# Later activation of the second layer's conditions, and three modulation chunks moved to later phases

## The reference

```python
m_lat = adaln_params(c, w_ada[i], b_ada[i])            # silu(c) @ w_ada + b_ada, six vectors of 1024
m_ctx = adaln_params(c_ctx[None], w_ada[i], b_ada[i])
a_lat = modulate_2(rms_norm(h_lat), m_lat[0], m_lat[1])
o_lat = mixer(a_ctx, a_lat)
h_lat = h_lat + m_lat[2] * o_lat
h_lat = h_lat + m_lat[5] * swiglu(modulate_2(rms_norm(h_lat), m_lat[3], m_lat[4]), ...)
```

## Time and profile before

| | |
|---|---|
| median of 3 runs | 1454.56 us (1452.75 to 1456.83) |
| the profiled execution, span | 1454.6 us |
| the profiled execution's own time | 1454.56 us, one of the three |
| PE busy | 1403.6 us, 96% of the span |
| DVE busy | 848.5 us, 58% |
| ACT busy | 659.0 us, 45% |
| POOL busy | 840.2 us, 58% |
| mean granted TensorE clock | 0.993 of full speed |

### The profile page before, as it was taken

How to read it: one execution, slowest core, us unless ns; L and a number is a source line. 1 busy time by engine, 2 the same in 40 slices (tenths; PEclk the granted TensorE clock), 3 DMA queues, 4 the chain that set the end, 5 groups by cost and what they waited for, 6 DMA issues and landing times.

```text
span 1454.6 us, 21621 instructions
## 1 busy us (share of the span) xinstructions
PE 1403.6 (96%) x8272; PEld 1172.3 (81%) x8272; DVE 848.5 (58%) x1638; ACT 659.0 (45%) x1070; POOL 840.2 (58%) x672
## 2 busy tenths in 40 slices
PE   5999999999999999999999999999999999999998
PEld 2978789999988888546878888888888866888887
DVE  3798667776676689688675333321126768554522
ACT  3555665455453133684342232232226386544442
POOL 1533427998864444675444554544446530699997
PEclk9999999999999999999999999999999999999999
DMA  9748516777775652010445555533333320365664
GB/s 365 288 164 309 195 50 212 248 258 241 243 259 194 202 192 80 31 44 15 174 174 182 195 202 185 193 122 96 102 107 102 110 94 16 118 200 188 187 187 135
DMA packets 71207, 242.01 MB, mean 166 GB/s; under 512 B 7488, under 2 KB 12992, under 8 KB 70720
## 3 DMA queue, kind: packets, MB, share of 16 engines
q1 hardware_dynamic: 68688, 236.63, 48.1%
q10 hardware_dynamic: 2416, 4.00, 0.9%
HBM read 238.50 MB, written 1.05 MB: 165 GB/s over the span
## 4 chain that ended last, share of the span: by engine, by line
PE 52%; DVE 4%; ACT 1%; issue 0%; POOL 0%; DVEq 0%; ACTq 0%
PE bank L731 9%; PE bank L737 9%; PE bank L732 9%; PE bank L593 8%; PE bank L594 4%; PE bank L584 2%; PE bank L586 1%; PE bank L585 1%; PE bank L592 1%; PE cond_a L1124 1%; PE bank L1124 1%; DVE h_both L2239 1%; PE bank L1132 1%; PE cond_a L1185 1%; PE bank L1144 1%; PE cond_b L1144 1%
## 5 line engine op out<-in xcount | busy, mean ns | idle before, releaser
L2010 POOL TENSOR_TENSOR w_lo<-raw,w_hi 128x512 fp32r<-128x512 f32 (+2 forms) x610 | 776.8, 1302 | 581.1 <-ACT w_hi L1466 572.9
L1466 ACT ACTIVATE w_hi<-raw 128x1024 fp32r<-128x1024 f32 (+3 forms) x300 | 307.9, 1029 | 582.7 <-PE bank L737 375.2
L731 PE MATMUL bank<-h_both,w_hi 128*128 128x512 f32 (+1 forms) x1000 | 323.1, 340 | 1.2 <-ACT w_hi L1466 1.2
L732 PE MATMUL bank<-h_both,w_hi 128*128 128x512 f32 (+1 forms) x1000 | 322.5, 340 | 0.0
L731 PEld LDWEIGHTS bank<-h_both,w_hi 128*128 128x128 f32 x1000 | 188.3, 188 | 22.9 <-ACT w_hi L1466 1.4
L732 PEld LDWEIGHTS bank<-h_both,w_hi 128*128 128x128 f32 x1000 | 188.3, 188 | 21.3
L737 PE MATMUL bank<-h_both,w_lo 128*128 128x512 f32 (+1 forms) x1000 | 198.1, 340 | 0.0
L737 PEld LDWEIGHTS bank<-h_both,w_lo 128*128 128x128 f32 x1000 | 160.4, 188 | 21.4 <-POOL w_lo L2010 0.2
L2124 DVE CUSTOM_DVE_ANT_0 ada_junk<-ada_w,cond_a 128x1024 bf16<-128x1024 f32 x128 | 153.5, 1215 | 15.1 <-DVE work L2687 8.1
L2106 DVE TENSOR_TENSOR hidden_both<-work,hidden_both 128x256 fp32r<-128x256 f32 (+1 forms) x66 | 58.5, 886 | 135.0 <-ACT hidden_both L1547 135.0
L593 PE MATMUL bank<-h_both,w_hi 128*128 128x512 f32 x345 | 122.8, 394 | 0.0
(11 more groups left out here) (487 smaller groups left out, 2544.1 us busy)
## 6 DMA issues: line engine op xcount, KB each, us to landing
raw<-in_up SPq DMA_DIRECT2D x132, 512.0 KB, 3.6
ada_w<-in_ada SPq DMA_DIRECT2D x128, 512.0 KB, 4.5
raw<-in_down SPq DMA_DIRECT2D x48, 448.0 KB, 3.5
raw<-in_out SPq DMA_DIRECT2D x24, 512.0 KB, 3.5
raw<-in_down SPq DMA_DIRECT2D x24, 512.0 KB, 3.6
raw<-in_in SPq DMA_DIRECT2D x24, 512.0 KB, 3.5
arena<-in_ada SPq DMA_DIRECT2D x16, 512.0 KB, 11.8
raw<-in_uq SPq DMA_DIRECT2D x12, 384.0 KB, 3.1
```

The lines of the kernel that those rows point to most:

```text
L731: pe.matmul(out, w_h[:, k - k0], hi[:, k, cols], start=(k == 0), stop=False)
L732: pe.matmul(out, w_h[:, k - k0], lo[:, k, cols], start=False, stop=False)
L1466: act.activation(part_slot(w_hi, f, u), raw_slot(f, u), ACT.Copy).then_inc(s["rounded"], 1)
L2010: pool.tensor_tensor(part_slot(w_lo, f, u)[:, a:b], raw_slot(f, u)[:, a:b], part_slot(w_hi, f, u)[:, a:b].bitcast(F32), ALU.subtract).then ...
```

## The change

Three things change. ACT activates layer 1's conditions after the norm behind `out0`, ahead of everything else of `up0`, where it did so ahead of `out0`. `out0` carries no chunk any more; `down0` carries one with every second unit up to unit 18, 10 in place of 8, and `in1` carries 23 in place of 22. In `down0` all chunks of a product now follow its residual.

```diff
 CARRIED = {"ka": (1, 2), "qa": (2, 1), "vma": (1, 2), "km": (1, 3), "vmb": (1, 2), "qm": (1, 1), "om": (1, 1),
-           "out0": (2, 1), "up0": (3, 1), "down0": (3, 1), "in1": (1, 1), "out1": (2, 1), "up1": (1, 1)}
-CARRY = {"out0": 6, "up0": 45, "in1": 22}
+           "up0": (3, 1), "down0": (2, 1), "in1": (1, 1), "out1": (2, 1), "up1": (1, 1)}
+CARRY = {"out0": 0, "up0": 45, "down0": 20, "in1": 23}
...
             round_next()
-            silu_cond(1)
             out_and_squares("out0", L0, L1)
             rms_std(L0, L1)
             rounded[0] += 1
             shift_h(0, 1, False)
+            silu_cond(1)
...
-                if u == 0 and f.name in ("ka", "out0", "out1"):
-                    dve.wait_ge(s["cond_ready"], {"ka": 1, "out0": 2, "out1": 3}[f.name])
+                if u == 0 and f.name in ("ka", "up0", "out1"):
+                    dve.wait_ge(s["cond_ready"], {"ka": 1, "up0": 2, "out1": 3}[f.name])
...
-                behind_k = {1: 0, 3: 2, 4: 4} if name == "out0" else {k: k for k in range(KD - 1)}
                 for k in range(KD):
-                    if k == KD - 1:
+                    if k == KD - 1 and name != "down0":
                         carried(f, units * k)
...
-                    if k in behind_k:
-                        carried(f, units * behind_k[k])
+                    if name == "down0":
+                        for u in range(units * k, units * (k + 1)):
+                            carried(f, u)
+                    elif k < KD - 1:
+                        carried(f, units * k)
```

## The result

| | before | with the change |
|---|---|---|
| median, 22 runs each on the same chip | 1456.09 us (1452.11 to 1460.37) | 1458.81 us (1454.03 to 1460.97) |
| the profiled execution, its own time and span | 1454.56, 1454.6 us | 1458.78, 1457.0 us |

The ratio is 1.0017, 95% interval 1.0009 to 1.0025: 2.5 us slower, 1.3 to 3.6. That is a little slower, and under the 0.3% that the prediction named as what can be told from no change. The forecast was 1456.2 us, +1.65 us on a base of 1454.56; the base itself came out at 1456.09 with more runs. So of the 2.6 us between forecast and median, 1.5 are the base and 1.1 the change. So what a change is worth is read from the whole times with their intervals, and a trace says where it may lie.

The account below looks back on a forecast made before the run. PE, busy in 96% of the span, bounds the kernel, so only its idle or slow places count. -2.2 + 0.85 + 0 + 2.6 + 0.4 = +1.65 us on 1454.56 us gave 1456.2 us, range 1452.4 to 1459.2 us.

Parts of the forecast that it names:

- Part 1: Start of out0 through its norm: without silu and chunks, rounding and the norm's inverse come earlier, -2.2 us (-1.8 to -2.9).
- part 2: Start of up0: silu there delays unit 3's rounding and POOL, so PE waits, +0.85 us (0.5 to 2.0).
- part 4: End of in1: the added chunk makes PE wait 5.15 us at vra, partly regained, net +2.6 us (2.28 to 5.15).
- the clock: Start of vra: half clock behind the new wait, none behind the transposes, net +0.4 us (-1.1 to +1.7).
- Part 3: down0: two more chunks cost 0 us, DVE being covered with 0.67 us to spare (-0.3 to +2.0).
- A table load costs the load alone: ACT's table switches: 1.28 us each without a drain; with the skill's drain, part 2 would be 1.4 us dearer.
- The slower rival: End of in1 and vra: the 5.15 us wait stands in full, clock stays low, +5.5 us, 1460.1 us; chance 0.10.
- a rival at +2.1 us: down0 becomes bound by its loads: six late units add 2.1 us to the forecast, 1458.3 us; chance 0.10.

Follow-up runs that it names:

- e5: Kernel before with the change's out0 and up0, down0 as before, the three chunks behind in1's products 2, 4 and 6: ratio 0.9991, -1.3 us.
- e2: The change with silu_cond(1) back ahead of out0, the chunks staying moved: 1459.9 us, 1.0022 of the kernel before.
- e4: The change with down0 as before, in1's extra chunks behind products 2, 4, 6, none behind 22, silu inside out0: 1454.13 us, 0.9981 of the kernel before.
- e6: Kernel before with one chunk of out0 moved to the end of in1, behind product 22: ratio 1.0020, +2.9 us.
- e9: Kernel before with sixteen chunks in down0 instead of eight, one in out0, sixteen in in1, the last behind product 15: 1456.22 us, ratio 1.0004.
- e10: e4 with in1's last chunk behind product 19, two more extra chunks behind products 8 and 10: 1450.80 us, 0.9967 of the kernel before.

## Why the prediction was right or wrong

That the change lies within 0.3%, and on which side, was right, and so were the sums for parts 1 with 2 and for part 4 with the clock, as far as the times can tell; behind both lie mechanisms that differ from the ones written down. Part 3's term was wrong.

- **Part 1 (-2.2) and part 2 (+0.85).** Right together: -1.35 against -1.3 us in e5 (0 to -2.8). In the trace, stage A gave 2.1 and 3.0 us in two executions, more than the forecast's 1.35, because the trace of before has the half-clock stretch of 226.30 to 229.70 in its norm. The prediction has no term for it, though it stands in the one trace that the prediction was read from; against the traces without it stage A gives 0.6 to 1.5 us. That the sum came out to a tenth is partly luck. Unit 5 came 1.76 us nearer to unit 3 (1.8 forecast), the wait at `up0`'s unit 3 was 0.32 us and POOL's late half 0.34 us (0.55 and 0.3 forecast). Two details were wrong: the inverse came at 223.91 as named, but from a start 0.8 us later, so 3.2 us earlier in `out0`'s own time, not 2.2 (2.0 in the change's second trace); and part of that was lost at once in a PE wait for POOL of 1.11 us that I hadn't looked for. The sentence that the chunks in `out0` cost only at the norm fits e2, which gives 0.3 us for all of them.
- **A table load costs the load alone.** The load at 232.13 starts 0.02 us after the activation at 231.60 ended, and the one at 236.40 starts 0.02 us after the rounding of 235.34 + 1.04. The Trainium skill, ScalarE: Activation LUTs, section "What ACT_TABLE_LOAD costs", has a drain of about 1380 ns on top of each switch; neither here nor in e4's row at 211.80 does ACT stand that long, and the measurement decides.
- **Part 4 (+2.6).** The price was right: the wait is 5.15 us to the hundredth, and the old 2.60 us came back. But it came back by another way than I wrote. I had `vra` take 12.0 us and DVE be ready only as it ended; in fact `vra` took 14.24 us (563.60 to 577.84), DVE's long products ahead of it ran faster than before (last section), and DVE waited 3.70 us for PE. The old wait is gone in either case.
- **The clock (+0.4).** It was low where forecast, from within the new wait to 568.4, for 6.9 us and not some 3.4. PE worked for 4.8 us of them, and `vra` took 2.2 us more than its 12.0: above my 1.2 to 1.7. What is given back is larger too: from the second transposes to line 1172 the change takes 17.64 us and the kernel before 19.83, 2.2 us less, where I had counted 1.1: the kernel before has a second half-clock stretch from 591.51, which the prediction didn't see and the change doesn't have. Both were mis-sized and nearly cancel, which is luck; part 4 and clock together are +2.58 us in stage E and +2.9 in e6, against 3.0. The Trainium skill, TensorE: Matmul & The Clock Gate, section "HAM oscillation — how this bites in real kernels", says that a gap sends the clock back and what follows starts cold; the row from 561.50 at 0.51 shows that, and e9 and e10, with no gap there, stay at 1.00. A gap isn't all there is to it here: e5 has the same 2.60 us wait at the transposes and a clock of 1.00 for the 16 us behind it, and the stretch from 591.51 has PE busy throughout.
- **The slower rival** (nothing comes back, clock low, 1460.1). Half of it happened: the long half-clock stretch and DVE waiting for PE. By its own condition, `vra` over 1.5 us longer than 12.0, it should have decided: it was 2.2 us longer. Its price was wrong: it left out that the old wait and the old half clock go all the same, because nothing at the transposes depends on PE having come early.
- **Part 3 (0).** This is the step that failed. "So DVE is covered" was right and beside the point. "Against: PE didn't stand, as nothing in its list of waits names a place in down0" was the error: a place with no wait before can be one unit from having one. "One raw load came late before" was a misreading too: the list has ACT waiting for raw loads seventeen times, 25.7 us in all, with the 3.30 us of the earlier trace rows as the longest. The case stood as a rival at +2.1 us. It measures +1.1 (stage C, mean of six traces) and +1.3 and +0.7 us (the same kernel twice, both intervals touching no change); only e9's +4.8 us for eight chunks is clear. With that the sum is 1.65 + 1.1 to 1.3 = +2.75 to 2.95, and the change measured +2.5 (1.3 to 3.6).

## What to carry to other kernels

Where a rounding engine has waited for transfers seventeen times in a stage and the main engine has not stood yet, the stage has little room for another load: price it above nothing (here 0.6 us a load, by e9's trace). When work can be put in any of several stages, look at which engine is behind at each stage's end: two pairs of sums cost 4.5 us of stage E behind `in1`'s products 20 and 21 and nothing that shows behind products 8 and 10 (e4 against e10), of which the whole time kept about 2 us. And an experiment whose whole time doesn't move may hold two effects of opposite sign; distances between stages in the traces showed 4.8 and -4.7 us where the times showed 0.5. Before such distances are compared, the granted clock in each of them has to be: one half-clock stretch made 1.2 to 1.7 us of difference here.

## What the runs showed of the hardware

**DVE and POOL took longer side by side.** The engines wait for each other only at semaphores, and yet two of them were slower while both were at work. The same DVE product, of the kernel before and of the change, and POOL's splitting at that time:

```profile
567.13 2.20 DVE L2801 TENSOR_TENSOR arena<-arena 128x1024 f32<-128x1024 f32 x1
```

```profile
566.40 7.52 POOL L2010 TENSOR_TENSOR w_lo<-raw,w_hi 128x512 fp32r<-128x512 f32 x4 [5.91 <-ACT w_hi L1466]
```

```profile
569.74 1.23 DVE L2803 TENSOR_TENSOR arena<-arena 128x1024 f32<-128x1024 f32 x1
```

```profile
571.73 2.77 POOL L2010 TENSOR_TENSOR w_lo<-raw,w_hi 128x512 fp32r<-128x512 f32 x2 [10.98 <-ACT w_hi L1466]
```

Beside POOL's work it took 2.20 us and POOL 1.88 us for a half of a unit; where POOL stood idle it took 1.23 us, and POOL by itself takes 1.27. In the change PE's delay had held back ACT's rounding and so POOL until DVE was through. Two such products, 2.1 us, are most of the lateness of DVE that made the old 2.60 us wait. That the overlap is the cause was not tried by itself; e9 and e10, where POOL is at work there too, have 2.19 us for that product. Their wait is gone all the same, because DVE enters these products earlier: 4.17 us behind `vra`'s start in e9, where it was 6.75.

**Clock and wait.** A wait of PE of 2.60 us was followed by 3.4 us at a granted clock of 0.51, and around one of 5.15 us it was 0.51 for 6.9 us. In six of seven traces with the 2.60 us wait the clock fell right behind it; in e5's it didn't. Over the whole run the change has a mean granted clock of 0.995 against 0.993, though it is slower.
